# Gates of a hybrid decoder step: the sigmoid moves from the reloaded rows to the eviction from PSUM

## The reference, cut to what matters

```python
u = _rms(x, norm_mix)
(dn_qkv, dn_z, dn_b, dn_a, r_q, r_k, r_v, r_g,
 a_q, a_k, a_v, i_q, i_k, i_w, gate) = _split_cols(jnp.einsum('bld,dc->blc', u, w_in))
...
br = jnp.stack([o_a.reshape(B, L, BRANCH_W), o_b.reshape(B, L, BRANCH_W),
                o_c.reshape(B, L, BRANCH_W)], axis=2)
br = jnp.einsum('blnc,ncd->blnd', br, w_branch)
gates = jax.nn.sigmoid(gate.reshape(B, L, N_BRANCH, D_MODEL))
h = x + jnp.einsum('bld,de->ble', jnp.sum(gates * br, axis=2), w_o)
```

## Time and profile before

| | us |
|---|---|
| median of 3 runs | 3123.01 |
| lowest, highest run | 3122.02, 3126.98 |
| profiled execution | 3118.19 |
| its span, first to last instruction | 3116.2 |
| TensorE busy | 2868.2 |
| VectorE busy | 1613.9 |
| ScalarE busy | 1171.4 |
| GpSimd busy | 786.4 |

### The profile page before, as it was taken

One profiled execution on the slowest core, in us unless ns is written; L12 is line 12 of the kernel. 1 busy time (PEld: TensorE's weight loads), 2 busy tenths in 40 slices (PEclk: granted clock), 3 DMA queues, 4 the chain that ended last, 5 costly groups with the idle time before them and its releaser, 6 DMA issues. The chain is left out here.

```text
span 3116.2 us, 56624 instructions
## 1 busy us (share of the span) xinstructions
PE 2868.2 (92%) x22439; PEld 2694.7 (86%) x22439; DVE 1613.9 (52%) x2463; ACT 1171.4 (38%) x2029; POOL 786.4 (25%) x364
## 2 busy tenths in 40 slices
PE   5998999998996999999979989999899869999998
PEld 4998988887885999999978889888788869999997
DVE  2363765654433639558225539455544235692861
ACT  2432434762212433334334314457422144332332
POOL 1231231220000433343322203122210024334331
PEclk8998899999985999999989979999999679999999
DMA  5221334543322623233242223255333235223323
GB/s 169 68 81 58 96 100 126 152 129 116 106 82 84 209 68 82 70 100 83 68 113 69 82 65 96 83 164 166 104 113 111 66 119 167 78 73 91 93 72 92
DMA packets 371413, 316.74 MB, mean 102 GB/s; under 512 B 47695, under 2 KB 321513, under 8 KB 370471
## 3 DMA queue, kind: packets, MB, share of 16 engines
q10 hardware_dynamic: 257332, 188.09, 20.1%
q1 hardware_dynamic: 113810, 124.96, 13.5%
HBM read 276.84 MB, written 36.15 MB: 100 GB/s over the span
## 5 line engine op out<-in xcount | busy, mean ns | idle before, releaser
L830 POOL TENSOR_TENSOR w_lo<-w_raw,w_hi 128x1024 fp32r<-128x1024 f32 (+2 forms) x360 | 786.2, 2187 | 2292.2 <-ACT w_hi L1471 2292.1
L837 PE MATMUL big<-uhi,w_hi 128*128 128x272 f32 x3712 | 1118.3, 301 | 40.2 <-DVE ulo L1982 31.4
L839 PE MATMUL big<-uhi,w_lo 128*128 128x272 f32 x3712 | 1083.0, 292 | 0.0
L838 PE MATMUL big<-ulo,w_hi 128*128 128x272 f32 x3712 | 1077.8, 290 | 0.0
L837 PEld LDWEIGHTS big<-uhi,w_hi 128*128 128x128 f32 x3712 | 709.4, 191 | 86.1 <-issue 47.1
L838 PEld LDWEIGHTS big<-ulo,w_hi 128*128 128x128 f32 x3712 | 710.9, 192 | 4.0 <-issue 1.9
L839 PEld LDWEIGHTS big<-uhi,w_lo 128*128 128x128 f32 x3712 | 708.4, 191 | 0.0
L1471 ACT ACTIVATE w_hi<-w_raw 128x1024 fp32r<-128x1024 f32 (+2 forms) x360 | 343.8, 956 | 404.7 <-PE big L839 332.3
L837 PE MATMUL big<-mhi,w_hi 128*128 128x272 f32 x640 | 191.5, 299 | 48.0 <-DVE mlo L2420 36.2
L837 PE MATMUL big<-hhi,w_hi 128*128 128x272 f32 x704 | 207.4, 295 | 4.3 <-DVE hlo L2524 4.3
L839 PE MATMUL big<-hhi,w_lo 128*128 128x272 f32 x704 | 204.9, 291 | 0.0
(11 more groups left out here) (348 smaller groups left out, 4206.9 us busy)
## 6 DMA issues: line engine op xcount, KB each, us to landing
w_raw<-in_w_in ACTq DMA_DIRECT2D x66, 1024.0 KB, 5.5
w_raw<-in_w_up ACTq DMA_DIRECT2D x88, 512.0 KB, 4.9
kpage<-in_cache_k SPq DMA_DIRECT2D x128, 256.0 KB, 3.0
w_raw<-in_w_down ACTq DMA_DIRECT2D x32, 704.0 KB, 4.8
d_conv<-in_cache_v SPq DMA_DIRECT2D x64, 256.0 KB, 2.7
d_pad<-in_cache_v SPq DMA_DIRECT2D x64, 256.0 KB, 2.7
gate_dram<-gate_raw ACTq DMA_DIRECT2D x48, 272.0 KB, 2.6
sig<-gate_dram SPq DMA_DIRECT2D x48, 272.0 KB, 3.3
```

Of the source, the lines that this page charges most:

```text
L830: po.tensor_tensor(split_view(lo, t), tile_of(t), split_view(hi, t).bitcast(F32), ALU.subtract).then_inc(w_lo.sem, w_lo.next(t))
L837: pe.matmul(out, wh, xh, start=start, stop=False)
L838: pe.matmul(out, wh, xl, start=False, stop=False)
L839: return pe.matmul(out, wl, xh, start=False, stop=stop)
```

## The change

The eviction of a gate goes through Sigmoid, so that gate_dram holds the gates themselves. ScalarE's sigmoid in the branch stage goes, all 24 calls of a layer, and VectorE waits for the reload of the row where it waited for ScalarE's sigmoid. The reloads by SP, the buffers and all else are as before.

```diff
             q = gate_no(u, i)
             if q:
                 ac.wait_ge(gate_stored.sem, gate_stored.at(q - 1))
-            copy_out(PJ[slot], ('gate', q), lambda x: [(halves(g.gate_raw[:, :]), x[:, :, 0:HT])])
+            copy_out(PJ[slot], ('gate', q), lambda x: [(halves(g.gate_raw[:, :]), x[:, :, 0:HT])], f=ACT.Sigmoid)
             ac.dma_start(g.gate_dram[q * P:q * P + P], g.gate_raw[:, :]).then_inc(
                 gate_stored.sem, gate_stored.next(q, 16))
...
         bsplit(0)
         bsplit(1)
-        def sigmoid(q):
-
-            s = g.sig[q % NSIG][:, :]
-            ac.wait_ge(gate_in[q % NSIG].sem, gate_in[q % NSIG].at(q))
-            act(s, s, ACT.Sigmoid).then_inc(act_out.sem, act_out.next(('sig', q)))
         def split_sum(k):
...
-        sigmoid(0)
-        sigmoid(1)
         for n in range(3):
             if n == 1:
                 bsplit(2)
             for d in range(4):
                 for j in range(2):
                     next_tile(f'br{n}{d}', j)
-                    q = br_no(f'br{n}{d}', j) + 2
-                    if q < 24:
-                        sigmoid(q)
                     if n == 2 and 1 <= 2 * d + j <= H:
                         split_sum(2 * d + j - 1)
...
                 for j in range(2):
                     k = 2 * d + j
-                    ve.wait_ge(act_out.sem, act_out.at(('sig', i)))
+                    ve.wait_ge(gate_in[i % NSIG].sem, gate_in[i % NSIG].at(i))
                     ve.wait_ge(PJ[j].filled, PJ[j].at(('br', i)))
```

## The result

The changed kernel took 3163.17 us (median of four runs, 3160.66 to 3164.93) against 3124.99 us of the kernel before in its four runs: a ratio of 1.0121, 95% interval 1.0104 to 1.0139, or +38 us (+32 to +43). The sum had said +38.7, the forecast 3161.

The account below looks back on a forecast made before the run. PE was taken as the bound, ScalarE counting only where PE waits. Gate loads of 7.7 + 18 + 8 + 7 less 2.0 for the branch stage gave +38.7 us, forecast 3161 us, 8-in-10 range 3143 to 3186.

Parts of the forecast that it names:

- What bounds the kernel: Whole kernel: PE busy 92% of the span, ScalarE 38%; ScalarE's work counts only where PE waits for it.
- The price of a load and its place: At the gates: each load starts when the bank is full and holds it 1.28 us longer; 54 more loads, 69.3 us.
- Rival (c): At the gates: loads run ahead of the fill and hide nearly all, -2 to +6 us, 3121 to 3129; chance 5%.
- rival (f): At every table switch: ScalarE held about another 1.28 us beyond the load, added terms double, 3202 us; chance 1%.
- Z, attention, DN, delta: Added time at the gates over both layers: Z +7.7 us, attention +18, DN +8, delta +7.
- the first prob's load: Attention, a table load ahead of the first softmax prob: 0.2 us a layer.
- rival (b): Attention and other gates: only banks held longer cost, reloads are hidden; +21 us, 3144; chance 13%.
- Rival (a): All stages: most loads are exposed, or the clock falls at new stalls; 3190 us; chance 17% with parts of it.
- the sum's own range: Total time of 3150 to 3175 us, with attention between 10 and 23, DN and delta between 8 and 20.
- The branch stage: Removed sigmoids save 0.56 us at the third branch's split and 0.45 at the tail: -1.0 a layer, -2.0 in all.
- Rival (d): Branch stage: ScalarE's sigmoids set the pace, so the kernel gets faster, about 3089 or 3112 us; chance 4%.
- The clock: PE's granted clock behind new stalls: nothing added, but up to 10 us for the upper end.

Follow-up runs that it names:

- e1: Kernel before with ScalarE's sigmoids and their table load removed, gates evicted with Copy, sigmoid left out altogether; 0.9993 of the kernel before, -2.2 us.
- e4: Changed kernel with one-column activations that load tables ahead of the waits of retention and attention gates and four decays; 1.0056 of the kernel before, +17 us.
- e7: Changed kernel with a one-column Sigmoid and Exp ahead of each Z gate's own Sigmoid, tile already there: three loads for one; 1.0221 of the kernel before, +69 us.
- e6: Changed kernel with Sigmoid in the eviction of the 4 attention gates a layer alone, other gates raw; 1.0067 of the kernel before, +21 us.
- e2: Changed kernel with ScalarE copying each row onto itself in the branch stage where it took the sigmoid; 1.0118 of the kernel before, +37 us.
- e3: Changed kernel with tanh(x/2) in the eviction, VectorE multiplying by (row + 1), factor 0.5 in the branch splits; 0.9996 of the kernel before, -1.2 us.
- e5: Changed kernel with Sigmoid in the eviction of the 8 DN gates a layer alone, other gates raw; 1.0034 of the kernel before, +11 us.

## Why the prediction was right, point by point

**What bounds the kernel.** Right. PE's new waits stand at the places named. e1 takes 34 us of work from ScalarE of the kernel before for some 2 us, and e4 adds 5 to that of the changed kernel and is 20 us faster. That ScalarE's sum rises by 38 us as well, by the count, is a coincidence.

**The price of a load and its place.** Right: 1.28 us each, after the fill. e4 shows the place by moving it, e7 the price by tripling it. Rival (c), loads ahead of the fill, is what e4 makes true by hand for twelve places a layer; rival (f), a dearer switch, is refuted by e7's timeline. The Trainium skill's drain of 1380 ns at a switch ("ScalarE: Activation LUTs", section "What ACT_TABLE_LOAD costs") shows in no run here: 0.02 us lie between load and activation.

**Z, attention, DN, delta.** Right to 0.1 us a step, but for the first prob's load, which had 0.2 us in each layer: it cost nothing in layer 1 and 0.52 in layer 2. In attention PE regains 0.43 and 0.32 us behind gates 0 and 2 in the softmax products, and that was in the numbers; rival (b), reloads hidden by the dense steps, is refuted by the lines for probT in e4 and e6. Rival (a), most loads exposed, is out by the table: of 69.3 us of loads 40.4 came through. Two bounds in the working were off: with the eight loads that the built order has in attention, 8 x 1.28 x 2 = 20.5 us would be the most there and not 23, and the terms named for the sum's own range give 3147 to 3172 and not 3150 to 3175. The forecast hangs on neither.

**The branch stage.** The direction was right and the tail mis-sized in the changed kernel: 1.8 to 2.0 us a layer for 1.0. (Of the 10.6 us that ScalarE waited ahead of its sigmoids, puts 9.2 to the rows and 1.4 to GpSimd's w_lo; the argument stands with 9.2.) The split gave its 0.55 us in layer 1 and 0.54 in layer 2. The tail gave 1.2 and 1.4 for 0.45, and mostly not through the sigmoids, since e2, which keeps ScalarE's place there, has 1.0 us of it in layer 1. In after, the cast of the first w_o tile waited 2.72 us for its weights; GpSimd's subtraction therefore came later, and VectorE's add in front of it ran at its short length (ScalarE, VectorE, GpSimd of after):

```profile
1102.85 1.06 ACT L1471 ACTIVATE w_hi<-w_raw 128x1024 fp32r<-128x1024 f32 x1 [2.72 <-DMA w_raw<-in_w_o]
...
1103.17 0.72 DVE L2436 TENSOR_TENSOR m<-m,sig 128x544 f32<-128x544 f32 x1
1104.01 2.95 DVE L2416 TENSOR_TENSOR mlo<-m,mhi 128x544 fp32r<-128x544 f32 x1
...
1103.99 8.03 POOL L830 TENSOR_TENSOR w_lo<-w_raw,w_hi 128x1024 fp32r<-128x1024 f32 x3 [3.02 <-ACT w_hi L1471]
```

In e1 the same add meets GpSimd and takes 2.91 us, and the low part behind it 2.83:

```profile
1077.49 2.91 DVE L2436 TENSOR_TENSOR m<-m,sig 128x544 f32<-128x544 f32 x1
1080.51 2.83 DVE L2416 TENSOR_TENSOR mlo<-m,mhi 128x544 fp32r<-128x544 f32 x1
...
1077.41 2.40 POOL L830 TENSOR_TENSOR w_lo<-w_raw,w_hi 128x1024 fp32r<-128x1024 f32 x1 [2.14 <-ACT w_hi L1471]
```

e1, e3, e4, e5 and e6 in both layers and e7 in layer 1, where that cast didn't wait for its weights, have 0.35 to 0.43 us less in the first of the tail's waits and give 0.17 to 0.22 of it back at the second. e7 in layer 2, where the cast waited 1.98 us for them, has the changed kernel's tail (2.56 less and 1.13 back), though both layers run the same program. So the sigmoids are worth 0.2 us of the tail and not 0.45, the branch stage some 0.75 a layer, and the rest in the changed kernel goes with where GpSimd's subtraction stood. Why the weights came later there was not tried, and in e2 the subtraction came late without such a wait. Rival (d), ScalarE pacing the branch stage, is refuted by e1.

**The clock.** I had added nothing, and one place in the changed kernel has a price. The wait ahead of the last product of attention grew from 1.0 to 2.2 us, and in layer 1 the granted clock behind it is 0.55 where it was 1.00; in DN it stayed at 1.00 behind a wait of 2.89 us. The stretches (columns as in the earlier trace rows) of that product and of the matmuls behind the s_log wait, both of after; then the first of them before; then the same product in e7 and the matmuls behind the s_log wait in layer 1 of e4; then, of after, PE's wait in DN and the product of layer 2:

```profile
515.10:518.90 3.80, 3.68 (x16) 3.49 (x16) 0.00 (x0) 0.60 (x1) 1.93 (x1) 0.55 0.00 0
716.00:722.00 6.00, 6.00 (x54) 5.64 (x53) 0.00 (x0) 2.41 (x4) 2.38 (x1) 1.00 0.14 49
...
500.90:503.00 2.10, 2.04 (x16) 1.85 (x16) 0.00 (x0) 0.56 (x1) 1.87 (x1) 1.00 0.00 0
...
528.80:531.00 2.20, 2.05 (x16) 1.86 (x16) 0.00 (x0) 0.62 (x2) 1.97 (x1) 1.00 0.00 0
...
702.37:705.87 3.50, 3.50 (x20) 3.49 (x21) 0.00 (x0) 3.00 (x6) 1.13 (x1) 0.64 0.24 84
...
715.11 1.20 PE L899 MATMUL aux<-consts,s_log 128*128 128x128 f32 x9 [2.89 <-DVE s_log L2260]
...
2066.42 2.05 PE L1104 MATMUL big<-probT,vtok 128*128 128x128 f32 x16 [2.23 <-ACT probT L1471]
```

The product of layer 1 keeps PE busy for 3.68 us where it was 2.04, so the fall costs 1.6 us. It repeats in e2 and e6, where that gate also has its load (0.56 and 0.58), and not in e4, where the load was hidden (1.00). But e7 has the same load and the same wait of 2.23 us and no fall (1.00), and in layer 2 no run has one; in after the product took 2.05 there. That DN had no fall in after was luck: behind nearly the same wait, 2.88 us, the clock over 3.5 us was 0.64 in layer 1 of e4, 0.69 in layer 2 of e5 and 0.53 in layer 2 of e7, and cost some 1.5 us each time. The reason given for adding nothing, that no new stall stands as long as 2.65 us, doesn't hold: the DN wait was itself forecast at 2.9 us, and a wait of 2.23 us was enough in attention. The sum's own range had room for it.

**The total.** 36.2 us of steps, 0.5 for the first prob of layer 2 and 1.6 of clock are 38.3, for a measured 38 (32 to 43). That the sum of +38.7 comes so near is in part luck. The branch stage gave 1.7 us more than the sum had, mostly by where GpSimd's subtraction stood, and the clock took 1.6 us for which the sum had nothing; the two cancel. The terms of the gates, 40.7 us in the sum and 40.4 by the steps, are not luck.

The two profiled executions differ by more, 3164.9 to 3118.2, 46.7 us. Some 8 of these lie outside the steps: 1.4 us of clock at the start of retention in layer 1 (e3 has it too, without any new load), 2.8 us in layer 1 and 0.3 in layer 2 between delta's last step and the split of the branch stage, 2.1 of them at one wait for ScalarE's d_pad (there e3 has 1.95, e4 0.1), and 3.3 us in the FFN of layer 1 and at the start of layer 2 (there e5, whose loads lie elsewhere, has 2.3). Two profiles can't tell a few us; the steps can, and the medians.

## What to carry to other kernels

Count the table loads that a new function brings, and then look in the built order for the wait that each has taken over: a load behind the wait for a full bank holds that bank for its whole 1.28 us, while the same load ahead of the wait cost PE nothing at the gates and the decays of e4. Before moving a function to another place, see whether its neighbours' table has a function that does the same (tanh for a sigmoid beside exp): that took back all 38 us. Removing 34 us from an engine that runs ahead gave some 2, within the noise.

## What the runs showed of the hardware that I had not expected

A wait of PE can cost more than its length: at the Z gates a wait of 1.23 us was followed by a granted clock of 1.00, one of 4.2 us by 0.62 in the next 3.5 us, and some 10 us of e7's time are of that kind. It is not the length alone. All six waits of 4.2 us were followed by a fall; the wait of 2.23 us at the end of attention was followed by one in three of its eight places (layer 1 of after, e2 and e6), and the wait of 2.88 us in DN in three of its ten (e4 in layer 1, e5 and e7 in layer 2). What else decides stays open.

VectorE's add of 544 columns took 0.72 us alone and 2.9 us when GpSimd's subtraction of a 128 x 1024 tile ran beside it, so that a late weight transfer made the tail of the branch stage shorter. Of the 48 adds and low parts (m and mlo) of after, the 15 beside which GpSimd did nothing took 0.72 to 0.73 us each, the other 33 up to 2.95.
